# A hybrid decoder layer: compact key norms, scores over four quadrants of the array, and down biases in row groups

## The chip, the cores and the metric

One core of one Trainium2 chip. The metric is the device time of one execution of the whole layer in microseconds (us), as the median of some runs. The engines are TensorE (PE, its weight loads PEld), VectorE (DVE), ScalarE (ACT), GpSimd (POOL) and SyncE (SP), which issues nearly all DMAs.

## The reference, cut to what matters

256 tokens of width 1024 pass one layer: an RMSNorm and one projection, whose columns go to an S5 state-space mixer (512) and to an RWKV-7 mixer (r, k, v, 512 each); an output projection; a mixture of 32 experts, four for each token; an embedding gated by the residual; a last norm. The parts that the change touches:

```python
kk = heads(k * k_k)                                   # 8 heads of 64
kk = kk / jnp.maximum(jnp.sqrt(jnp.sum(kk * kk, axis=-1, keepdims=True)), 1e-12)
...
sa = jnp.einsum('bhvk,bhk->bhv', state, neg_kk_t)     # rwkv7_step, token by token
state = (state * w_t[:, :, None, :] + sa[..., None] * kka_t[:, :, None, :]
         + v_t[..., None] * k_t[:, :, None, :])
...
yb = act @ w_down[e] + b_down[e]                      # moe_ffn, for the tokens that chose e
return yb.astype(f32) * gw[:, None]
```

The kernel computes the RWKV scan in chunks of 64 tokens. Within a chunk the recurrence becomes products of 64x64 matrices ("scores") and a triangular inverse.

## The kernel before, in words

`layer` is one block in which each engine has its own instruction list in a fixed order; semaphores are the only links. At its end all engines meet, a short second block (router) follows, they meet again, and a third block loops over the experts. Its ring of eight 2 MB slots (`RING`) in SBUF is filled by SP; slots 0, 4, 5, 1 are loaded in the first block, 2, 3, 7 at the start of the second, 6 at the start of the third, and from then on a slot is refilled when the expert's matmuls have read it (`refill`, L1386).

The first block, on PE: projections 0 to 3, the small projections (`lora`), per-head sums of the squared keys (`head_sums(kksq, 4)`, two matmuls with 512 columns), projections 4 and 5, `kernel_taps`, `turn_g` (32 transposes into banks 2 to 5 that ACT copies out, L468), `stack_u` and `into` (S5), projections 6 and 7. Key norms: DVE divides with a reciprocal of all 1024 columns (L706). Then the RWKV part. A unit is one pair of heads in one chunk, 16 units in all; `pair` (L241) does two 64x64 matmuls for it, one for each head, on partitions 0 to 63 and 64 to 127, whose results lie on the same partitions of one bank:

```python
for h in range(2):
    a = slice(h * CH, (h + 1) * CH)
    last = mm(out[a], lhsT[a], rhs[a], start, stop)
```

Five sets of scores (L1008) give X, Mx, KA, RB, RK; DVE copies each out with its mask (L739). Five levels of a block inverse (L1033) follow: 16 pairs W = MO X, ACT copies them (L477), 16 pairs with Y, DVE adds them to X (L781) and transposes. `turn` (transposes of Bs, Ks, Vs) and `s5_out` (the S5 result) are placed between the levels. Then four chunks c of the scan proper (L1099) with `glu` and `project_out` in between, group norm, and the output projection. POOL splits the experts' gate and up biases into parts (L340 to L344); ACT waits for it before the last tile.

The second block: the last transposes, `ple_proj`, router logits, top four, ranks, gates; PE transposes the gates to 32 rows (L1351), and four matmuls with 32 rows and 512 columns start the output banks with the down biases (L1357). PE needs `p_in` for `ple_proj(0)`, two DMAs issued in the first block; DVE needs `router_in`, the router's bias, which SP issues first in this block (L1246).

Every fp32 matmul stands in the trace as two passes, so the counts of PE in the rows are twice those of the program.

## Time and profile before

| | |
|---|---|
| median of 3 runs | 1209.59 us (1205.43 to 1210.69) |
| the profiled execution | 1203.81 us, its span 1202.0 us |
| PE busy | 1076.2 us, 90% |
| DVE, ACT, POOL busy | 365.5, 176.3, 17.5 us |
| TensorE clock granted | 0.991 of 2.4 GHz |
| HBM read | 428.70 MB, 358 GB/s over the span |
| instructions | 18872 |

Times of rows are microseconds from the start of the span. A row of the timeline merges instructions of one line and form that follow each other: start, length, engine, line, operation, out<-in, shapes, count, and in brackets the idle time before it and what ended it.

### The profile page before, as it was taken

How to read it: one execution, taken by the hardware profiler on the slowest of the kernel's cores; microseconds unless marked ns; L12 is line 12 of the kernel's file. 1: busy time of each engine (PE TensorE's matmuls, PEld its weight loads, DVE VectorE, ACT ScalarE, POOL GpSimd, SP SyncE). 2: the span in 40 equal slices, each digit the busy share in tenths (PEclk: the TensorE clock that was granted, in tenths of full speed). 3: DMA queues.
4: the chain of work that ended last, by engine and by line, in shares of the span. 5: the costliest groups of instructions: out<-in, count | busy, mean ns of one | idle time of the engine just before them, and what ended most of it. 6: DMA issues, size and time to landing. Idle time of an engine off the chain costs nothing. (4 is left out here: it accounts for less than half of the span.)

```text
span 1202.0 us, 18872 instructions
## 1 busy us (share of the span) xinstructions
PE 1076.2 (90%) x8132; PEld 492.5 (41%) x8132; DVE 365.5 (30%) x739; ACT 176.3 (15%) x288; POOL 17.5 (1%) x18
## 2 busy tenths in 40 slices
PE   6989998899999988888888888888888888888896
PEld 5779884443334333333333333333333333333342
DVE  5997925522222111111222111111111221211122
ACT  5580231400000000000000000000000000000023
POOL 0000005000000000000000000000000000000000
PEclk9989999899999999999999999999999999999999
DMA  9301184589999999999999999999999999999970
GB/s 324 125 2 37 43 328 142 211 359 426 428 428 430 428 429 428 427 428 429 429 429 430 428 429 428 428 428 430 429 429 428 429 428 428 427 430 428 430 289 35
DMA packets 44531, 430.28 MB, mean 358 GB/s; under 512 B 4912, under 2 KB 15536, under 8 KB 19920
## 3 DMA queue, kind: packets, MB, share of 16 engines
q1 hardware_dynamic: 44304, 429.24, 85.5%
q8 instruction: 28, 0.46, 0.2%
q0 software_dynamic: 192, 0.52, 0.1%
q14 instruction: 7, 0.06, 0.0%
HBM read 428.70 MB, written 1.05 MB: 358 GB/s over the span
## 5 line engine op out<-in xcount | busy, mean ns | idle before, releaser
L1221 PE MATMUL bank<-arena 128*64 128x512 f32 (+5 forms) x5136 | 847.3, 467 | 91.0 <-DMA arena<-in_exp_w_up 58.3
L1221 PEld LDWEIGHTS bank<-arena 128*64 128x64 f32 (+4 forms) x5136 | 307.8, 128 | 607.0 <-issue 446.2
L239 PE MATMUL bank<-arena 64*64 64x64 f32 (+7 forms) x2048 | 161.6, 264 | 15.4 <-ACT arena L362 8.5
L239 PEld LDWEIGHTS bank<-arena 64*64 64x64 f32 (+3 forms) x2048 | 129.3, 144 | 45.7 <-issue 26.3
L1410 ACT ACTIVATE arena<-arena 128x512 f32<-128x512 f32 x32 | 20.1, 630 | 520.2 <-DVE arena L1458 520.2
L1463 DVE TENSOR_SCALAR arena<-bank 128x512 f32<-128x512 f32 x32 | 22.1, 691 | 227.7 <-PE bank L1221 227.7
L1473 DVE COPY arena<-bank 128x512 f32<-128x512 f32 x32 | 22.1, 691 | 202.8 <-PE bank L1221 202.8
L1458 DVE TENSOR_SCALAR arena<-bank 128x512 f32<-128x512 f32 x32 | 22.1, 691 | 194.0 <-PE bank L1221 194.0
L1413 ACT ACTIVATE arena<-bank 128x256 f32<-128x256 f32 x32 | 12.3, 383 | 326.2 <-PE bank L1517 326.2
L1434 DVE TENSOR_TENSOR arena<-bank,par 128x512 f32<-128x512 f32 x33 | 22.8, 691 | 77.9 <-PE bank L1221 77.9
L1466 DVE SCALAR_TENSOR_TENSOR arena<-arena 128x512 f32<-128x512 f32 x32 | 33.7, 1052 | 1.1
L1461 DVE TENSOR_TENSOR arena<-arena 128x512 f32<-128x512 f32 x32 | 22.1, 692 | 24.5 <-ACT arena L1410 24.5
L1415 ACT ACTIVATE arena<-bank 128x512 f32<-128x512 f32 x32 | 19.1, 597 | 1.7
L1521 PE MATMUL bank<-con,arena 128*128 128x128 f32 x128 | 19.2, 273 | 0.0
L1446 DVE TENSOR_SCALAR arena<-con,arena 128x128 f32<-128x128 f32 x64 | 19.1, 340 | 0.1
L1431 DVE TENSOR_SCALAR arena<-con,arena 128x64 bf16<-128x64 f32 x66 | 13.8, 251 | 14.3 <-PEq L1243 7.5
L1517 PEld LDWEIGHTS bank<-con,arena 128*128 128x128 f32 x64 | 6.5, 141 | 24.3 <-issue 24.3
L1521 PEld LDWEIGHTS bank<-con,arena 128*128 128x128 f32 x128 | 15.0, 140 | 0.0
L239 PE MATMUL bank<-arena,con 128*32 128x64 f32 (+1 forms) x144 | 11.4, 322 | 3.6 <-ACT arena L506 1.4
L1517 PE MATMUL bank<-con,arena 128*128 128x128 f32 x64 | 14.1, 301 | 0.0
L1410 ACT ACT_TABLE_LOAD x8 | 10.3, 1283 | 7.8 <-PEq L1243 7.7
L352 ACT ACTIVATE arena<-par 128x2048 f32<-128x2048 f32 (+1 forms) x7 | 10.3, 1533 | 0.0
(275 smaller groups left out, 406.7 us busy)
## 6 DMA issues: line engine op xcount, KB each, us to landing
arena<-in_exp_w_gate SPq DMA_DIRECT2D x64, 2048.0 KB, 32.2
arena<-in_exp_w_down SPq DMA_DIRECT2D x64, 2048.0 KB, 35.4
arena<-in_exp_w_up SPq DMA_DIRECT2D x64, 2048.0 KB, 35.3
arena<-in_w_in SPq DMA_DIRECT2D x8, 1024.0 KB, 12.9
arena<-in_w_out SPq DMA_DIRECT2D x4, 1024.0 KB, 6.3
arena<-in_ple_w_gate SPq DMA_DIRECT2D x2, 2048.0 KB, 33.4
arena<-in_xT SPq DMA_DIRECT2D x1, 1024.0 KB, 6.0
arena<-in_lora SPq DMA_DIRECT2D x1, 1024.0 KB, 13.6
```

The costliest lines, as they stand in the source:

```text
L239: return nc.tensor.matmul(out, lhsT, rhs, start=start, stop=stop, skip_group_check=True)
L1221: return nc.tensor.matmul(out, lhsT, rhs, start=start, stop=stop, skip_group_check=True)
L1410: nc.scalar.activation(sg, gt, ACT.Sigmoid, scale=1.702).then_inc(s["sig_ready"], 1)
L1415: nc.scalar.activation(actT[:, :, :, :], GATE[:, :].rearrange("p (k h s) -> p k h s", h=2, k=4), ACT.Copy).then_inc(s["actT_ready"], 1)
L1434: tt(xg[:, :, :], GAT[:, :].rearrange("p (k s) -> p k s", k=KD), prm("g_moe_run")[:, :, None].to_broadcast([P, KD, SLOTS]), ALU.mult).then ...
L1458: ts(gt, GATE[:, :], 7.0, None, ALU.min).then_inc(s["gt_ready"], 1)
L1461: tt(sg, sg, gt, ALU.mult).then_inc(s["swish_ready"], 1)
L1463: ts(up, UP[:, :], 7.0, -7.0, ALU.min, ALU.max).then_inc(s["up_read"], 1)
L1466: stt(by_run(gt), plain(up), 1.0, plain(sg), ALU.add, ALU.mult).then_inc(s["act_ready"], 1)
L1473: V.tensor_copy(y, YB[:, :]).then_inc(s["y_ready"], 1)
L1517: last = nc.tensor.transpose(YB[:, t * P:(t + 1) * P], pg[:, t, :], ident)
L1521: last = nc.tensor.transpose(GATE[:, k * P:(k + 1) * P], gt[:, k * P:(k + 1) * P], ident)
```

## The change

Three parts. *Front:* the squared keys are summed with the data as weights and two columns of ones (`head_pair`), which gives 16 columns; DVE inverts those; 16 matmuls with a broadcast weight spread them over 1024 columns again. The order of the front is new: `turn_g` in two halves behind the sums and behind the spread, `kernel_taps` behind projection 5; ACT takes a part of two token shifts, POOL two memsets. *Four quadrants:* units 8 to 15 (chunks 2 and 3) get the halves crossed, so that four 64x64 matmuls can be in different quarters of the array; this holds for scores and turns; in chunks 2 and 3 the scan crosses back, and waits (`first_half`) stand between two halves of one sum. ACT copies three score sets, POOL masks RB and RK, `phase_on(1)` moves ahead of the levels, the head sums of `rk` behind the first W, the last `s5_out` behind the last W. *Down biases:* gates and biases lie in four groups of 32 rows; the router's bias DMA counts on `p_in`, and PE waits for all three.

```diff
+        gfirst = un(9).rearrange("p (m j c) -> p m j c", m=2, c=32)
+        head_pair = head_ones[:, 0:P:CH]
+        norms, rest_mu = u0[:, 0:4 * TT * 2], u0[:, 32:32 + 2 * FT].rearrange("p (m f) -> p m f", f=FT)
-        bias_down = un(42)[0:E, :]
+        bias_down = un(42)[:, 0:D // 2]
...
-                a = slice(h * CH, (h + 1) * CH)
-                last = mm(out[a], lhsT[a], rhs[a], start, stop)
+                a, o = slice(h * CH, (h + 1) * CH), slice((h ^ cross) * CH, (h ^ cross) * CH + CH)
+                last = mm(out[o], lhsT[a], rhs[a], start, stop)
...
-                sp.dma_start(bias_down, io["exp_b_down"]).then_inc(bias_in, 16)
+                for r in range(4):
+                    hf = r % 2
+                    sp.dma_start(bias_down[r * E:(r + 1) * E, :], io["exp_b_down"][:, hf * 512:(hf + 1) * 512]).then_inc(bias_in, 16)
...
+                pool.wait_ge(s["proj_done"], at_place[0])
+                nc.gpsimd.memset(EL, 1.0).then_inc(s["pool_set"], 1)
...
+                nc.gpsimd.memset(un(2, 2), 0.0).then_inc(s["pool_set"], 1)
...
+                        pool.wait_ge(s["scores_moved"], 2 * n + b + 3)
+                        nc.gpsimd.tensor_tensor(d, d, causal, ALU.mult).then_inc(s["scores_masked"], 1)
...
+                        A(gfirst[a, m, :, o], gprod[m][a, 0], ACT.Copy)
+                        A(gpad[m][a, :, :, o].rearrange("p j n c -> p n j c"), gprod[m][a], ACT.Copy).then_inc(s["padded"], 1)
...
+                act.wait_ge(s["kk_summed"], 1)
+                A(norms, banks[6][:, 0:4 * TT * 2], ACT.Sqrt).then_inc(s["kk_norm"], 1)
...
-                    m = A(kb[:, 2 * b:2 * b + 2, :], banks[4 + b].rearrange("p (f t) -> p f t", t=T), ACT.Sqrt)
...
-                clear(2, 2)
+                for n in range(4, 8):
+                    copy_g(n)
...
+                for m, dst in ((1, Mx), (3, RB), (4, RK)):
+                    for b in range(2):
+                        act.wait_ge(s["scores_done"], 2 * m + b + 1)
+                        A(dst[:, 8 * b:8 * b + 8, :], banks[SCORE_BANK[m] + b].rearrange("p (u t) -> p u t", t=CH), ACT.Copy).then_inc(s["scores_moved"], 1)
...
-                link(ts(kb, kb, 1e-12, None, ALU.max))
-                link(V.reciprocal(kb, kb))
-                link(tt(kkn, kkn, kb, ALU.mult))
+                dve.wait_ge(s["kk_summed"], 2)
+                for b in range(2):
+                    d = kkn[:, 2 * b:2 * b + 2, :]
+                    last = tt(d, d, banks[6 + b].rearrange("p (f t) -> p f t", t=T), ALU.mult)
...
-                head_sums(kksq, 4).then_inc(s["kk_summed"], 1)
+                for n in range(4 * TT):
+                    tok = slice(n // FT * P, (n // FT + 1) * P)
+                    last = mm(banks[6][:, 2 * n:2 * n + 2], kksq[:, n % FT, tok], head_pair, True, True)
+                last.then_inc(s["kk_summed"], 1)
+                turn_g(0)
                 project(4)
+                pe.wait_ge(s["kk_norm"], 2)
+                for n in range(4 * TT):
+                    tile, f = n // FT, n % FT
+                    for h in range(2):
+                        last = mm(banks[6 + f // 2][h * CH:(h + 1) * CH, (f % 2) * T + tile * P:(f % 2) * T + (tile + 1) * P],
+                                  norms[:, 2 * n + h:2 * n + h + 1].to_broadcast([P, CH]), ident, True, True)
+                last.then_inc(s["kk_summed"], 1)
+                turn_g(1)
                 project(5)
...
+                    for u in range(8):
+                        o = slice(u * CH, (u + 1) * CH)
+                        ins = pair(banks[bank][:, o], fm(l, u), fm(r, u))
...
+                        last = pair(banks[bank + 1][:, o], fm(l, u + 8), fm(r, u + 8), cross=True)
...
-                pe.wait_ge(s["xy_ready"], 2 * LEVELS)
                 pe.wait_ge(s["turned"], 6)
                 pe.wait_ge(s["bonus_ready"], 1)
+                pe.wait_ge(s["scores_masked"], 4)
...
+                    if cross:
+                        pe.wait_ge(s["first_half"], 3 * c - 4)
                     for i, o in enumerate(tiles):
-                        last = pair(banks[0][:, o], fm(at, c * FT + i), state[:, o], False, True)
+                        last = pair(banks[0][:, o], fm(at, c * FT + i), state[:, o], False, True, cross)
...
-            sp.dma_start(rbias[:, :], io["router_b"].to_broadcast([P, E])).then_inc(s["router_in"], 16)
+            sp.dma_start(rbias[:, :], io["router_b"].to_broadcast([P, E])).then_inc(p_in, 16)
...
-            pe.wait_ge(p_in, 32)
+            pe.wait_ge(p_in, 48)
             ple_proj(0, banks[0]).then_inc(s["ple_done"], 1)
...
-            for tile in range(TT):
-                last = nc.tensor.transpose(banks[5][0:E, tile * P:(tile + 1) * P], gates[:, tile, :], ident)
+            rows = [slice(n * E, (n + 1) * E) for n in range(4)]
+            for n in range(4):
+                last = mm(banks[5][rows[n], 0:P], gates[:, n // 2, :], ident, True, True)
...
-                mm(banks[n][:, :], gatesT[:, n // 2 * P:(n // 2 + 1) * P], bias_down[:, n % 2 * HF:(n % 2 + 1) * HF], True, False)
+                mm(banks[n][:, :], gatesT[rows[n], :], bias_down[rows[n], :], True, False)
```

In the expert loop only the name of a semaphore changes (`up_read` goes, its count is added to `swish_ready`).

PE in the front, from the small projections' second part to the S5 matmuls (`arena`, `con`, `lora_hidden`, `rec` are SBUF tensors, `bank` is PSUM, counts are matmuls). Before:

```order
L239 MATMUL bank<-lora_hidden,arena 128x256 x4
L239 MATMUL bank<-arena,con 128x512 x2
L239 MATMUL bank<-arena 128x256 x32
L239 MATMUL bank<-arena 32x32 x4
...
L894 MATMUL bank<-con,arena 128x128 x32
L239 MATMUL bank<-arena,con 32x64 x64
```

and now:

```order
L242 MATMUL bank<-lora_hidden,arena 128x256 x4
L242 MATMUL bank<-con,arena 128x2 x8
L948 MATMUL bank<-con,arena 128x128 x16
L242 MATMUL bank<-arena 128x256 x16
L242 MATMUL bank<-con,rec 64x128 x16
L948 MATMUL bank<-con,arena 128x128 x16
L242 MATMUL bank<-arena 128x256 x16
L242 MATMUL bank<-arena 32x32 x4
```

The 32 transposes stood in one piece behind the taps; they now stand in two pieces of 16, each with a projection behind it.

ACT at the same place, before:

```order
L441 ACTIVATE arena<-bank 128x512 x2
L448 ACTIVATE arena<-arena 64x64x16 x4
L352 ACTIVATE arena<-par 128x2048
...
L463 ACTIVATE arena<-bank 32x16x32 x4
L468 ACTIVATE arena<-bank 128x512 x8
```

and now:

```order
L438 ACTIVATE arena<-bank 128x512 x4
L485 ACTIVATE arena<-arena 64x64x16 x4
L438 ACTIVATE arena<-bank 128x512 x4
L415 ACTIVATE arena<-bank 128x512
L490 ACT_TABLE_LOAD
```

The eight copies of `turn_g` (L468, now L438) stood behind the sine tables and the taps; they stand ahead of both, four on each side of the pads, and the memset of 2048 columns (L352) is POOL's.

PE from the fifth score set to the second level, before:

```order
L239 MATMUL bank<-arena 64x64 x160
L239 MATMUL bank<-arena,con 128x512 x2
L239 MATMUL bank<-arena 64x64 x64
L239 MATMUL bank<-arena 128x256
```

and now:

```order
L242 MATMUL bank<-arena 64x64 x192
L242 MATMUL bank<-arena,con 128x512 x2
L242 MATMUL bank<-arena 64x64 x32
L242 MATMUL bank<-arena 128x256
```

160 are the scores, 32 more the W of the first level: the two head sums of `rk` stand behind W instead of ahead of it.

## Rows read from the trace of the kernel before

**Rows 1.** The page: granted clock and DMA share in 40 equal slices.

```profile
PEclk9989999899999999999999999999999999999999
DMA  9301184589999999999999999999999999999970
```

**Rows 2.** Windows: busy time of each engine (and count), granted clock, DMA share, GB/s.

```profile
core 0: us, PE busy (x) PEld busy (x) DVE busy (x) ACT busy (x) POOL busy (x), PEclk, DMA share, GB/s
76.40:81.00 4.60, 0.05 (x1) 0.05 (x1) 4.50 (x4) 4.54 (x9) 0.00 (x0) 0.90 0.00 0
81.00:84.60 3.60, 3.60 (x20) 3.27 (x23) 3.60 (x5) 3.05 (x6) 0.00 (x0) 0.50 0.00 0
109.50:121.70 12.20, 11.45 (x325) 10.09 (x324) 10.79 (x20) 0.60 (x1) 0.00 (x0) 1.00 0.28 90
232.90:241.00 8.10, 6.46 (x8) 2.14 (x8) 0.60 (x4) 0.45 (x1) 0.00 (x0) 0.55 0.78 331
241.00:244.70 3.70, 2.74 (x49) 2.59 (x49) 0.86 (x3) 0.84 (x1) 0.00 (x0) 0.60 0.75 261
244.70:248.60 3.90, 3.90 (x18) 1.38 (x20) 1.04 (x7) 0.00 (x0) 0.00 (x0) 1.00 0.69 294
248.60:1150.00 901.40, 814.78 (x5097) 302.98 (x5094) 180.03 (x407) 59.95 (x103) 0.00 (x0) 1.00 1.01 428
```

**Rows 3.** The timeline, SP and PE: router's bias, `ple_proj(0)`, expert 0, first refill.

```profile
221.76 0.34 SPq L1246 DMA_DIRECT2D arena<-in_router_b  x1
...
222.70 1.88 PE L1221 MATMUL bank<-arena,lora_hidden 128*128 128x512 f32 x4
...
248.62 3.68 SPq L1389 DMA_DIRECT2D arena<-in_exp_w_up  x2
```

**Rows 4.** The timeline of the front: ACT's pads, PE's head sums, taps, transposes, stack.

```profile
47.78 4.29 ACT L427 ACTIVATE arena<-arena 64x1024 f32<-64x1024 f32 x4
...
56.76 1.96 PE L239 MATMUL bank<-arena,con 128*128 128x512 f32 x4 [0.91 <-ACT arena L410]
...
72.46 1.82 PEld L239 LDWEIGHTS bank<-arena 128*32 128x32 f32 x128 [0.33 <-issue]
...
74.42 1.97 PE L894 MATMUL bank<-con,arena 128*128 128x128 f32 x16
...
80.95 3.68 PE L894 MATMUL bank<-con,arena 128*128 128x128 f32 x16 [4.56 <-ACT arena L468]
...
84.56 3.10 PE L239 MATMUL bank<-arena,con 128*32 128x64 f32 x128
```

**Rows 5.** The timeline of scores and levels: DVE and ACT around PE's 64x64 matmuls.

```profile
110.74 0.69 DVE L748 TENSOR_TENSOR arena<-bank,con 128x512 f32<-128x512 f32 x1 [4.09 <-PE bank L239]
...
114.87 1.10 DVE L755 TENSOR_SCALAR arena<-arena,par 128x256 f32<-128x256 f32 x4
...
122.92 0.60 ACT L477 ACTIVATE arena<-bank 128x512 f32<-128x512 f32 x1 [12.67 <-PE bank L239]
...
129.56 3.71 PE L239 MATMUL bank<-arena 64*64 64x64 f32 x119 [1.09 <-issue]
...
133.07 2.06 PE L239 MATMUL bank<-con,arena 64*64 64x64 f32 x64
...
158.38 1.15 PE L239 MATMUL bank<-arena 64*64 64x64 f32 x32 [0.79 <-DVE arena L781]
...
158.95 1.06 ACT L483 ACTIVATE arena<-arena 128x1024 f32<-128x1024 f32 x1 [1.28 <-DVE arena L661]
```

**Rows 6.** The timeline around POOL's bias parts: DVE's group norm, tile 0 and tile 1.

```profile
198.31 2.45 POOL L343 TENSOR_TENSOR arena<-arena 32x1024 f32<-32x1024 f32 x1
...
198.81 3.64 DVE L808 TENSOR_SCALAR arena<-arena,par 128x128 f32<-128x128 f32 x4
...
207.93 1.11 DVE L808 TENSOR_SCALAR arena<-arena,par 128x128 f32<-128x128 f32 x4
```

**Rows 7.** DMA issues: the router's bias, KB each, median us from issue to landing.

```profile
arena<-in_router_b SPq DMA_DIRECT2D x1, 16.0 KB, 3.1
```

More of the change, by code:

```diff
@@ L412, in lora_out, with copy_g, rest_of_shift @@
                             last.then_inc(s["lora2_copied"], 1)
+                def copy_g(n):
+                    m, q = n // 4, n % 4
+                    act.wait_ge(s["g_turned"], n + 1)
+                    A(gturn[m][:, 4 * q:4 * q + 4, :], banks[2 + q].rearrange("p (j q) -> p j q", q=P), ACT.Copy).then_inc(s["g_copied"], 1)
+                def rest_of_shift(m, src, dst, signal):
+                    act.wait_ge(s["eps_ready"], 2)
+                    for i in range(FT):
+                        last = A(dst[:, i, :], src[:, i, :], ACT.Copy, scale=rest_mu[:, m, i:i + 1])
+                    last.then_inc(s[signal], 1)
                 copy_proj(0)
+                clear(9, 1)
                 copy_proj(1)
@@ L464, in _ @@
                 last.then_inc(s["taps_ready"], 1)
-                for m in range(2):
-                    for q in range(4):
-                        act.wait_ge(s["g_turned"], 4 * m + q + 1)
-                        A(gturn[m][:, 4 * q:4 * q + 4, :], banks[2 + q].rearrange("p (j q) -> p j q", q=P), ACT.Copy).then_inc(s["g_copied"], 1)
                 for b in range(2):
@@ L671, in token_shift, with add_shifted @@
                     return m
-                dve.wait_ge(s["proj_copied"], at_place[5])
-                dve.wait_ge(s["lora1_done"], 2)
-                link(token_shift("k", kx))
+                def add_shifted(m, name, dst):
+                    dve.wait_ge(s["shift_rest"], m + 1)
+                    for i in range(FT):
+                        last = stt(dst[:, i, 1:T], raw[name][:, i, 0:T - 1], prm("mu_" + name)[:, i:i + 1], dst[:, i, 1:T], ALU.mult, ALU.add)
+                    return last
+                link(add_shifted(0, "k", kx))
                 for i in range(FT):
@@ new lines, in _ @@
+                for b in range(2):
+                    dve.wait_ge(s["scores_done"], b + 1)
+                    d = X[:, 8 * b:8 * b + 8, :]
+                    link(tt(d, banks[SCORE_BANK[0] + b].rearrange("p (u t) -> p u t", t=CH), col(C_SU1), ALU.mult))
+                    link(tt(d, d, eye, ALU.add))
+                    turn_x(b).then_inc(s["scores_copied"], 1)
+                for b in range(2):
+                    dve.wait_ge(s["scores_moved"], b + 1)
+                    level_mask(0, b)
@@ L762, in value_and_bonus @@
+                for b in range(2):
+                    dve.wait_ge(s["scores_done"], 4 + b + 1)
+                    tt(KA[:, 8 * b:8 * b + 8, :], banks[SCORE_BANK[2] + b].rearrange("p (u t) -> p u t", t=CH), col(C_SU), ALU.mult).then_inc(s["scores_copied"], 1)
+                phase_on(1)
                 def value_and_bonus():
                     dve.wait_ge(s["proj_copied"], 8)
-                    token_shift("v", vv).then_inc(s["scaled"], 1)
+                    add_shifted(1, "v", vv).then_inc(s["scaled"], 1)
@@ L1029, in turn @@
                     pe.wait_ge(s["scaled"], 4)
-                    for b in range(2):
-                        if n:
-                            pe.wait_ge(s["turned"], 2 * n - 2 + b + 1)
-                        for u in range(8 * b, 8 * b + 8):
-                            last = pair(banks[b][:, (u % 8) * CH:(u % 8 + 1) * CH], fm((bh, kh, vv)[n], u), con[:, C_ID2:C_ID2 + CH])
-                        last.then_inc(s["turn_done"], 1)
+                    if n:
+                        pe.wait_ge(s["turned"], 2 * n)
+                    arr, eye = (bh, kh, vv)[n], con[:, C_ID2:C_ID2 + CH]
+                    for u in range(8):
+                        o = slice(u * CH, (u + 1) * CH)
+                        ins = pair(banks[0][:, o], fm(arr, u), eye)
+                        if u == 7:
+                            ins.then_inc(s["turn_done"], 1)
+                        last = pair(banks[1][:, o], fm(arr, u + 8), eye, cross=True)
+                    last.then_inc(s["turn_done"], 1)
                 for lev in range(LEVELS):
@@ L1102, in _ @@
                     for i, o in enumerate(tiles):
-                        pair(banks[0][:, o], KA[:, c * FT + i, :], Vs[:, c * FT + i, :], i == 0, False)
+                        last = pair(banks[0][:, o], KA[:, c * FT + i, :], Vs[:, c * FT + i, :], i == 0, False)
+                    if cross:
+                        last.then_inc(s["first_half"], 1)
                     if c:
@@ L1115, in _ @@
                     for i, o in enumerate(tiles):
-                        pair(banks[5][:, o], state[:, o], fm(rt, c * FT + i), False, False)
+                        last = pair(banks[5][:, o], state[:, o], fm(rt, c * FT + i), False, False)
+                    if cross:
+                        last.then_inc(s["first_half"], 1)
                     pe.wait_ge(s["u0_ready"], c + 1)
+                    pe.wait_ge(s["xy_ready"], 2 * LEVELS)
                     for i, o in enumerate(tiles):
@@ L1551, in _ @@
         def _(dve):
[L1552 removed]
+            link = chain(dve, "dve")
             def finish(t):
```

199 lines of the change are left out of this document (105 added, 94 removed).

## The prediction

> **What bounds the kernel now.** I read the slices first: the DMA share goes up and down, with slices near 0, in the first eight slices of 30 us and stays at 9 from the tenth on, while PE's clock falls below 9 in two slices only, the third and the eighth [rows 1]. The windows say what each stretch waits for. The expert loop, 248.60 to 1150.00, moves 428 GB/s at a DMA share of 1.01 with PE busy for 814.78 of 901.40 us: it is bound by transfers, and the change leaves them alone. So the loop keeps its length and moves as a whole with its first refill, which SP issues at 248.62 [rows 2, 3]. That refill waits for expert 0's first matmuls, 244.70 [rows 3], and these for everything ahead. Ahead of it PE, DVE and ACT hand work round and the DMAs have gaps, so a microsecond saved on that chain is one saved at the end, as long as the transfers keep up: in 232.90 to 248.60 they are idle for 8.10 x 0.22 + 3.70 x 0.25 + 3.90 x 0.31 = 3.9 us [rows 2].
>
> The timeline of each stretch that the diff touches comes last. In the front, PE idles 4.56 us for ACT's copies of the first 16 transposes; behind that the granted clock is 0.50, the lower level of 1.2 GHz, and the second 16 take 3.68 us where the first took 1.97 [rows 2, 4]. In the scores, DVE is busy for 10.79 of 12.20 us and PE's windows end on it: five sets of 1.9 each (as 64 passes of the turns) and the `rk` sums of 1.96 fill the time, and the first W waits for DVE's masks [rows 2, 4, 5]. In the second block the clock is at 0.55, and the four down-bias matmuls (eight passes) take 6.46 us [rows 2].
>
> Each fp32 matmul is two passes. 32 matmuls of 64x64 are 64 passes, 2.06 us [rows 5]: 64 ns for two passes, since the halves of a pair already run side by side.
>
> **A, the front: -4.4.** Removed: the idle of 4.56 (the copies now have two projections to hide behind) and, as no such idle precedes, the low clock: transposes 3.68 - 1.97 = 1.7, the S5 stack 3.10 - 1.9 = 1.2 (nearest full-clock row: 128 taps, whose weights load in 1.82) [rows 4]. Gain 7.5, by 4.56 + 2.9. Added: four more pads on ACT, a quarter as long as the four of 4.29, 1.1, with the fixed cost of four more instructions 1.3, which PE's norm sums wait for; 16 matmuls of 64x128 to spread the norms, 32 passes at about 0.11 where the two heads of a pair overlap (16 transposes are 1.97, so 0.12 each): 16 x 0.11 = 1.8; without overlap 3.5. The old sums with 512 columns, 1.96 [rows 4], are replaced by 8 with two columns and by transposes that had to be done anyway: about 0. DVE's division of 1024 columns goes; it lay beside PE's projections, so 0. ACT's shift parts, POOL's memsets: beside PE, 0. +1.3 + 1.8 - 4.6 - 2.9 = -4.4. Bounds: -7.5 (nothing added is seen) and +1 (another copy is waited for, the idle only moves).
>
> **B, scores to the first W: -4.3.** Before: 109.50 to 121.70 is 12.2 us [rows 2]. Now PE needs 0.95 for X's whole set, as four quadrants work, 0.25 of hand-over, DVE's work on X 4.1 (110.74 to 114.87, [rows 5]), 0.1, the set that reuses X's banks 0.93, 0.25, two copies on ACT 2 x 0.60 [rows 5], 0.1: 7.9. DVE no longer copies the sets on this path, and the `rk` sums (1.96 by the like row, [rows 4]) come behind W.
>
> **C, levels: -1.9.** Three turns of 2.06 go to 1.0: -3.0. The wait of 0.79 for DVE ahead of 158.38 is filled by `s5_out`: -0.8. The idle of 1.09 ahead of 129.56, which has no named releaser, goes with `phase_on(1)`: -1.1. The `rk` sums arrive: +1.9. The last `s5_out` comes late, so the gelu of 1.06 (158.95) is no longer hidden, and `glu(0)` waits for it: +1.1 [rows 5]. The chunks' `first_half` waits stand where PE changes sides: no row shows such a wait, bounds 0 and 8 x 0.33 (the "issue" gap, [rows 4]); I take one, **+0.3**, since the second half mostly starts behind other work.
>
> **D, group norm: -0.7.** Four `L808` take 3.64 while POOL's 2.45 runs, and 1.11 without [rows 6]: a stall of 2.5. As block 1 is earlier at this place, and POOL's chain hangs on other things, the overlap may be less or the same. Bounds 0 and -2.5; I take a little over a quarter, since the few us by which block 1 is earlier here are small beside POOL's whole chain.
>
> **E, the router's bias: +2.1.** PE's `ple_proj(0)` starts at 222.70. It now waits for a DMA issued at 221.76 that takes 3.1 [rows 3, 7]: 224.86, so 2.1 later, if I put its landing that way; nothing hides it, for behind it on PE stand the logits' transposes, which DVE's top four wait for. Bounds 0 (the transfer lands sooner) and 2.5.
>
> **F, down biases: -4.6.** 6.46 for eight passes is 0.81 each [rows 2]. Four groups of 32 rows side by side take as long as one matmul: 2 x 0.81, with starts 1.7. Two more small matmuls for the gates cost 0.2. 1.7 + 0.2 - 6.46 = -4.6. The taps, which lie on tiles of 32 columns, need 1.82 for 128 [rows 4], 14 ns each: tiles do run four wide; for tiles of 32 rows no row shows it. Bounds 0 and -4.8. The Trainium skill, TensorE: Matmul & The Clock Gate, Measured speedup vs the span model, gives 3.07 for four row groups with 512 columns, an estimate of 2.1 in place of 1.7; the sum would be 0.4 less. No run here shows it yet.
>
> **G, the start of expert 0: +1.0.** With 5 us less of matmuls ahead of it, the clock (0.60 in 241.00 to 244.70) may rise later. One clock level costs the 3.90 us of 244.70 to 248.60 once more at most: 0 to +3.9; a quarter, as this stretch is at 1.00 right from its start [rows 2].
>
> **H, POOL's masks and memsets beside DVE: +0.5.** In [rows 6] DVE lost about as long as POOL ran. Four masks of 512 columns, half of the 1024 that took 2.45, are 4.9: bounds 0 and 4.9. I take a tenth, since they run beside the first W, where PE has the `rk` sums to do meanwhile.
>
> **Sum:** -4.4 - 4.3 - 1.9 + 0.3 - 0.7 + 2.1 - 4.6 + 1.0 + 0.5 = **-12.0**. The profiled execution takes 1203.8 us, so 1191.8; the median shown is 1209.59, higher by 5.8, and the forecast against it is 1209.6 - 12.0 = **1197.6**. Of the 12, what falls behind the start of block 2 (E, F, G: -1.5) is under the 3.9 us that the transfers leave.
>
> **Rivals.** *R1, the quadrants stay two wide.* For it: no row shows two matmuls on the same rows of the array for different columns at 64x64; against: the 32-column taps do run that way [rows 4]. Two score sets on the path cost 0.93 more each, three turns 1.05 each: +5.0, 1202.6. What rows show of sharing is that both halves of a pair, on different rows, write the same bank within one 64 ns step [rows 5]. The Trainium skill, TensorEngine Tiling (Array Packing), Restrictions and Gotchas, says that different row tiles cannot access the same PSUM bank at once; the trace of the pairs does not agree, and so I take nothing from it. By that rule the crossed half would wait like the straight one, which is R1's time. Chance 0.13.
>
> *R2, the row groups run one after the other:* F gives +0.2 in place of -4.6: 1202.4. For it, that no row shows 32-row tiles; against, [rows 5] with 64-row tiles side by side. 0.08.
>
> *R3, slower: the clock stays low into the experts.* Now PE's 6.46 us of work at 0.55 is followed by a clock that has risen by 244.70 [rows 2]. With 1.7 us there, PE is mostly idle in block 2's end, and expert 0 could run at 1.2 GHz. An expert is 814.78/32 = 25.5 us of PE at full clock, 51 at the low one, against 901.4/32 = 28.2 of transfers: 23 us late per expert [rows 2]. It takes 12.0 to use up the gain and 18 to be slower by more than 0.5%, that is three quarters of expert 0 at the low clock: 1209.6 - 12.0 + 23 = 1220.6. Against it: expert 0 keeps PE busy without a break, and at 81.00 the low clock, too, ended within 7 us of busy PE [rows 2, 4]. 0.05.
>
> *R4, the transfers are the bound already:* a transfer behind which the refill queues keeps its place in time though the chain is earlier. With only 3.9 us of idle at the end, and shares of 0.28 and less in the scores [rows 2], savings before the ring's loads count only if these loads move up as well. Their issue waits for SBUF that the same chain frees, which speaks against. Half the gain would be lost: 1203.6, no change. 0.07.
>
> *R5, better than the sum:* the idle in A goes and nothing added is seen (3.1 more), E lands early (2.1): 1192.4. 0.05.
>
> **How the numbers follow.** The main case has 0.62, with its own spread of about 5 us either way (A's and E's bounds). The range leaves out R3 and the tails of R4 and R5: 1190 to 1205. A measurement here can tell about 0.5%, 6.05 us: faster is under 1203.5. Main, R1, R2, R5 and the lower part of R4 give faster 0.83; the other part of R4 and the upper tails same 0.12; R3 slower 0.05.
>
> **What would show it.** No idle of PE near 76 and clock at full from 80 to 88; first W some 8.7 us earlier (A and B); turns at about 1.0; `ple_proj(0)` released by the router's bias DMA about 3 us after block 2 starts; the four bias matmuls in some 1.7; first refill near 236.6; loop still 901 long. Wrong if the loop's length changes, if the turns still take 2.06, if the bias matmuls take over 3, or if the clock is low behind 235.

## The result and the profile after

The change makes the kernel slower: 1215.70 us (1207.41 to 1220.63, 20 runs) against 1207.40 us (1203.58 to 1210.69, 20 runs) in the same series, a ratio of 1.0066 with a 95% interval of 1.0053 to 1.0079. The forecast was 1197.6.

The profiled execution of the changed kernel has a span of 1215.9 us, that of before 1202.0. The first execution (1217.66 us) is 2.0 us above its kernel's median, the second (1203.81) 3.6 under its own, so the two traces differ by more (13.9) than the kernels do (8.3).

The page's slices of the changed kernel, clock and DMA share:

```profile
PEclk9997999889999999999999999999999999999998
DMA  9300166379999999999999999999999999999960
```

Before there were two slices below 9 [rows 1]; now there are four, and the fourth slice, 91 to 122 us, is at 7. Windows of the changed kernel (busy time of PE, PEld, DVE, ACT, POOL, then clock, DMA share, GB/s):

```profile
core 0: us, PE busy (x) PEld busy (x) DVE busy (x) ACT busy (x) POOL busy (x), PEclk, DMA share, GB/s
90.00:106.80 16.80, 16.80 (x72) 16.17 (x73) 9.79 (x16) 0.78 (x1) 0.00 (x0) 0.50 0.00 0
234.79:247.81 13.02, 13.02 (x31) 7.47 (x31) 6.32 (x21) 4.81 (x9) 0.00 (x0) 0.54 0.98 416
261.90:1163.30 901.40, 814.66 (x5093) 302.95 (x5090) 180.15 (x407) 59.90 (x102) 0.00 (x0) 1.00 1.01 428
```

The last line is the loop's window of [rows 2], moved by the 13.3 us by which the first refill is later: the same work at the same rate fits into it. From the first refill to the end of the span it is 954.0 us, 953.4 before, so all but 0.6 of the difference lies ahead of it. The timeline of PE (and two lines of SP) shows where; columns as in [rows 4]:

```profile
47.91 2.00 PE L242 MATMUL bank<-lora_hidden,arena 64*128 64x256 f32 x16
...
60.83 2.16 PE L242 MATMUL bank<-con,arena 128*128 128x2 f32 x16 [2.09 <-ACT arena L430]
62.86 3.35 PE L948 MATMUL bank<-con,arena 128*128 128x128 f32 x16
...
73.05 1.97 PE L242 MATMUL bank<-con,rec 128*64 128x128 f32 x32
74.94 1.97 PE L948 MATMUL bank<-con,arena 128*128 128x128 f32 x16
...
88.75 0.43 PE L242 MATMUL bank<-arena,con 128*32 128x64 f32 x16 [1.41 <-issue]
89.90 32.24 PE L242 MATMUL bank<-arena 128*128 128x64 f32 x320 [0.72 <-ACT arena L504]
...
127.63 1.49 PE L242 MATMUL bank<-arena 64*64 64x64 f32 x42 [0.17 <-ACT arena L517]
129.90 0.85 PE L242 MATMUL bank<-arena 64*64 64x64 f32 x22 [0.78 <-issue]
...
140.94 1.15 PE L242 MATMUL bank<-con,arena 64*64 64x64 f32 x62
...
154.74 1.90 PE L242 MATMUL bank<-arena 64*64 64x64 f32 x58 [0.70 <-issue]
...
158.55 7.27 PE L242 MATMUL bank<-arena 64*64 64x64 f32 x228 [0.80 <-issue]
...
167.35 1.99 PE L242 MATMUL bank<-arena 128*128 128x256 f32 x8 [1.06 <-ACT arena L527]
...
204.25 7.76 PE L242 MATMUL bank<-arena 128*128 128x512 f32 x16
213.85 10.57 PE L242 MATMUL bank<-arena 128*128 128x512 f32 x24 [1.84 <-DVE arena L865]
...
231.69 0.34 SPq L1338 DMA_DIRECT2D arena<-in_router_b  x1
...
234.79 3.78 PE L1311 MATMUL bank<-arena,lora_hidden 128*128 128x512 f32 x4 [1.99 <-DMA arena<-in_router_b]
238.37 3.46 PE L1311 MATMUL bank<-arena 128*128 128x32 f32 x16
241.63 6.18 PE L1311 MATMUL bank<-arena,lora_hidden 128*128 128x512 f32 x8
...
249.61 1.14 PE L1311 MATMUL bank<-arena 32*128 32x512 f32 x8 [0.41 <-ACT arena L1365]
...
255.72 6.78 PE L1311 MATMUL bank<-arena 128*64 128x512 f32 x20 [0.87 <-DVE arena L1526]
...
261.91 3.68 SPq L1481 DMA_DIRECT2D arena<-in_exp_w_up  x2
```

The starts of matching instructions in the two traces divide the 13.3 us by which the first refill is later (261.91 against 248.62):

| stretch, from start to start | before | after | difference | forecast |
|---|---|---|---|---|
| span's start to the small projections' second part | 45.03 | 47.91 | +2.9 | 0 |
| from there to `into` | 43.36 | 41.99 | -1.4 | -4.4 (A) |
| `into` and projections 6, 7 to the first score | 21.15 | 29.21 | **+8.1** | 0 |
| first score to first W | 12.2 | 8.5 | -3.7 | -4.3 (B) |
| first W to `glu(0)` | 38.3 | 39.7 | +1.4 | -1.9, H +0.5 |
| `glu(0)` to the last `project_out` with S5 inputs | 35.7 | 36.9 | +1.2 | +0.3 |
| from there to block 2 | 26.0 | 27.5 | +1.5 | -0.7 (D) |
| block 2's start to expert 0 | 22.9 | 24.0 | +1.1 | -2.5 (E, F) |
| expert 0 to the first refill | 3.9 | 6.2 | +2.3 | +1.0 (G) |

### The profile page after: what moved, and what is told of

Read it like the earlier page. It is cut to its first block and busy times, and to the rows that moved or that the text cites. A ratio compares the mean times of both kernels' runs of the same rounds, so it can differ in the third digit from the quotient of the medians.

```text
span 1215.9 us, 18973 instructions
## 1 busy us (share of the span) xinstructions
PE 1085.2 (89%) x8182; PEld 498.8 (41%) x8182; DVE 358.5 (29%) x726; ACT 183.1 (15%) x309; POOL 26.9 (2%) x25
## 5 line engine op out<-in xcount | busy, mean ns | idle before, releaser
L242 PE MATMUL bank<-arena 64*64 64x64 f32 (+7 forms) x2048 | 170.5, 272 | 20.5 <-ACT arena L382 8.5
L242 PEld LDWEIGHTS bank<-arena 64*64 64x64 f32 (+3 forms) x2048 | 135.4, 150 | 53.2 <-issue 35.4
L1507 ACT ACTIVATE arena<-bank 128x512 f32<-128x512 f32 x32 | 19.1, 597 | 1.7
L1523 DVE TENSOR_SCALAR arena<-con,arena 128x64 bf16<-128x64 f32 x66 | 13.9, 252 | 9.0 <-DVE arena L1544 6.8
L1311 PE MATMUL bank<-arena,lora_hidden 128*128 128x512 f32 x16 | 11.9, 900 | 2.0 <-DMA arena<-in_router_b 2.0
L415 ACT ACTIVATE arena<-bank 128x512 f32<-128x512 f32 x8 | 5.8, 720 | 35.0 <-PE bank L242 35.0
```

What stands on the lines that cost most here:

```text
L242: return nc.tensor.matmul(out, lhsT, rhs, start=start, stop=stop, skip_group_check=True)
L1311: return nc.tensor.matmul(out, lhsT, rhs, start=start, stop=stop, skip_group_check=True)
L1507: nc.scalar.activation(actT[:, :, :, :], GATE[:, :].rearrange("p (k h s) -> p k h s", h=2, k=4), ACT.Copy).then_inc(s["actT_ready"], 1)
```

## The experiments

Each run was timed against the kernel before on the same chip in the same series (medians of before 1205.5 to 1209.1), so ratios to before are what is compared across series. Two theories to begin with. **C, the clock:** PE's short idle times bring the low level, and what PE does there counts double. **W, the waits:** what is lost are the added waits and the clash of POOL and DVE themselves.

### The router's bias gets its own wait again

```diff
-            sp.dma_start(rbias[:, :], io["router_b"].to_broadcast([P, E])).then_inc(p_in, 16)
+            sp.dma_start(rbias[:, :], io["router_b"].to_broadcast([P, E])).then_inc(s["logits_done"], 16)
...
-            act.wait_ge(s["logits_done"], 1)
+            act.wait_ge(s["logits_done"], 17)
...
-            dve.wait_ge(p_in, 48)
-            dve.wait_ge(s["logits_done"], 1)
+            dve.wait_ge(s["logits_done"], 17)
...
-            pe.wait_ge(p_in, 48)
+            pe.wait_ge(p_in, 32)
```

> The changed kernel, but PE's ple_proj(0) waits only for the two early DMAs, as before, and DVE alone waits for the router's bias. Theory C (the clock): in the changed kernel PE idles 1.99 us for this DMA and the granted clock is at the low level from there on, so that ple_proj and the logits take 3.78 + 3.46 + 6.18 = 13.4 us where they took 7.5 before; with the wait gone both go: 1215.7 - 2.0 - 5.9 = about 1208. Theory W (the wait itself): only the 2.0 go, the clock falls anyway: about 1213.7. No effect: 1215.7.

Measured: 1208.62 us, ratio 1.0022 (1.0008 to 1.0036), so 0.0044 or some 5 us under the changed kernel's. The trace, PE in the second block:

```profile
234.18 1.88 PE L1311 MATMUL bank<-arena,lora_hidden 128*128 128x512 f32 x4
236.17 1.97 PE L1311 MATMUL bank<-arena 128*128 128x32 f32 x16
237.98 3.68 PE L1311 MATMUL bank<-arena,lora_hidden 128*128 128x512 f32 x8
```

The wait is gone and the 13.4 us are 7.5 again. A wait of 2 us cost about 5 (3 to 8 by the two intervals): C, not W, which had 2.

### POOL's masks go to DVE

```diff
-                for n, dst in enumerate((RB, RK)):
-                    for b in range(2):
-                        d = dst[:, 8 * b:8 * b + 8, :]
-                        pool.wait_ge(s["scores_moved"], 2 * n + b + 3)
-                        nc.gpsimd.tensor_tensor(d, d, causal, ALU.mult).then_inc(s["scores_masked"], 1)
...
+                    if lev in (1, 2):
+                        for b in range(2):
+                            d = (RB, RK)[lev - 1][:, 8 * b:8 * b + 8, :]
+                            dve.wait_ge(s["scores_moved"], 2 * lev + b + 1)
+                            tt(d, d, col(C_UI), ALU.mult).then_inc(s["scores_masked"], 1)
```

> The changed kernel, but DVE masks RB and RK, in the second and third level, where it has idle time, and POOL does nothing in the scores. In the changed kernel DVE's operations beside POOL's four masks took 1.64 to 1.76 us in place of 0.69. Theory P (POOL and DVE hinder each other): some 4 us of DVE come back, of which about 3 lie on the path: about 1212.7. Rival: DVE had slack there, the added masks (4 x 0.69) cost as much: 1215 to 1217.

Measured: 1215.04 us, 1.0062 (1.0040 to 1.0085): no change against 1.0066. The clash is real. In the changed kernel a DVE operation beside POOL's masks takes 1.76 us:

```profile
127.24 6.48 POOL L352 TENSOR_TENSOR arena<-arena,con 128x512 f32<-128x512 f32 x4 [68.36 <-ACT arena L517]
127.48 1.76 DVE L708 TENSOR_TENSOR arena<-arena 128x512 f32<-128x512 f32 x1
```

In this run DVE's operations are back to 0.69 us, but DVE then waits for PE instead:

```profile
130.14 0.69 DVE L789 TENSOR_TENSOR arena<-arena,con 128x512 f32<-128x512 f32 x1 [0.49 <-PE bank L242]
133.14 0.69 DVE L829 TENSOR_TENSOR arena<-arena,bank 128x512 f32<-128x512 f32 x1 [2.31 <-PE bank L242]
```

Theory P falls: no cost of H can be seen in the time.

### The crossing is switched off

```diff
-                a, o = slice(h * CH, (h + 1) * CH), slice((h ^ cross) * CH, (h ^ cross) * CH + CH)
+                a, o = slice(h * CH, (h + 1) * CH), slice(h * CH, (h + 1) * CH)
```

> The changed kernel with the crossing switched off: the halves of units 8 to 15 go to the same side as those of units 0 to 7, everything else (order, waits between halves of a sum, ACT copies) stays. Theory Q (four quadrants do work side by side, as the turns' 1.15 us in place of 2.03 say): three turns and two score sets go back to two wide, +3 and +1.8: about 1220. Rival (the waits of the scan and DVE eat the gain, or PE is not the bound there): 1215 to 1217.

Measured: 1218.20 us, 1.0092 (1.0061 to 1.0122), against 1.0066: +3, but the intervals overlap. In the trace the turns are back at the old length:

```profile
147.15 2.03 PE L242 MATMUL bank<-con,arena 64*64 64x64 f32 x64
```

1.15 against 2.03 us shows four 64x64 matmuls side by side. From the first score to the first W this trace takes 10.2 us where the changed kernel takes 8.5, so the crossing wins 1.7 there, as the theory says. From the first W to `glu(0)` it takes 39.4 us, and the changed kernel 39.7: the 2.6 us that three shorter turns save do not show. PE has 1.07 us of idle there with straight halves and 3.34 with crossed ones. What the quadrants are worth was asked again without the new front (below).

### The row groups alone, in the kernel before

```diff
+            rows = [slice(n * E, (n + 1) * E) for n in range(4)]
+            for n in range(4):
+                last = mm(banks[5][rows[n], 0:P], gates[:, n // 2, :], ident, True, True)
...
-                mm(banks[n][:, :], gatesT[:, n // 2 * P:(n // 2 + 1) * P], bias_down[:, n % 2 * HF:(n % 2 + 1) * HF], True, False)
+                mm(banks[n][:, :], gatesT[rows[n], :], bias_down[rows[n], :], True, False)
```

with the four DMAs and POOL's count of 192 as in the change.

> The kernel before with the down biases in four row groups as the only change (the router's bias keeps its own semaphore). The changed kernel's trace shows 1.14 us for the four where before it was 6.46, so -5.3, and +0.1 for two more small matmuls: 1207.4 - 5.2 = about 1202. Rival: with less work for PE ahead of the experts the clock rises later, and the first expert gives back 2 to 4 us: 1204 to 1206.

Measured: 1204.53 us, 0.9989 (0.9974 to 1.0005): almost nothing won. In the trace the eight passes are down to 1.50 us, but the group norm ahead of them is late:

```profile
205.44 12.26 PE L239 MATMUL bank<-arena 128*128 128x512 f32 x24 [2.40 <-DVE arena L813]
...
236.14 1.50 PE L1223 MATMUL bank<-arena 32*128 32x512 f32 x8 [0.40 <-ACT arena L1275]
```

Before, this wait was 1.16 and the 24 passes took 10.57. POOL waits for all bias DMAs, the four for the down biases among them, although it never reads these. The rival that was named for this run shows as well: from expert 0's start to the first refill this trace takes 5.9 us, 3.9 before, at a low clock that before fell on the down biases.

### POOL no longer waits for the down biases

One edit, on the kernel with the row groups alone and on the changed kernel with its router wait mended:

```diff
-                    sp.dma_start(bias_down[r * E:(r + 1) * E, :], io["exp_b_down"][:, hf * 512:(hf + 1) * 512]).then_inc(bias_in, 16)
+                    sp.dma_start(bias_down[r * E:(r + 1) * E, :], io["exp_b_down"][:, hf * 512:(hf + 1) * 512]).then_inc(p_in, 16)
...
-                pool.wait_ge(bias_in, 192)
+                pool.wait_ge(bias_in, 128)
...
-            pe.wait_ge(p_in, 32)
+            pe.wait_ge(p_in, 96)
```

> e4_bias_alone (the kernel before with row groups alone), and POOL no longer waits for the down biases. In e4 the second block came 3.2 us later than before (PE idle 2.40 for DVE, then 12.26 for 10.57 at a low clock), which ate the 5.0 won by the row groups. Theory L: these 3.2 come back: 1204.5 - 3.2 = about 1201.3. Rival: the loss has another cause: 1204.5.

> e1_router_wait, and POOL starts its bias parts when the gate and up biases are there, no longer waiting for the four DMAs of the down biases (they count on the semaphore that PE waits for in the second block). Theory L (late POOL): in e1 PE idles 2.90 us for DVE L865 and its next 24 passes take 13.50 us in place of 10.57, since POOL's 1024-column operations now lie on tile 0's group norm; earlier POOL gives back 1.7 of idle and the 2.9 of low clock: about 4.5 under e1, 1204. Rival: POOL's chain is long enough (15 us) to meet the group norm either way: within 1 us of e1, 1208.6.

Measured, old front: 1203.66 us, 0.9967 (0.9951 to 0.9982); with 0.9989 ahead of it, 2.7 us came back, and the row groups are worth 4.0 us (2.2 to 5.9) once POOL is out of the way. The 2.7 are no more than an estimate, since the intervals overlap, and not all of it need be POOL's: in the two traces 3.0 us are won ahead of the second block, but expert 0 is also back at 3.9 us. Changed kernel: 1209.08 us, 1.0006 (0.9990 to 1.0021), 1.9 less than e1, with overlapping intervals too. There the group norm still meets POOL, as these rows of DVE and POOL show, first of the changed kernel, then of e5:

```profile
205.14 2.12 POOL L363 TENSOR_TENSOR arena<-arena 64x1024 f32<-64x1024 f32 x1
...
205.25 2.56 DVE L860 TENSOR_TENSOR arena<-arena 128x512 f32<-128x512 f32 x1
207.84 4.49 DVE L862 TENSOR_SCALAR arena<-arena,par 128x128 f32<-128x128 f32 x4
```

```profile
187.09 1.04 POOL L360 CAST arena<-arena 128x1024 bf16<-128x1024 f32 x1 [61.43 <-DMA arena<-in_exp_b_up]
...
198.61 4.50 DVE L862 TENSOR_SCALAR arena<-arena,par 128x128 f32<-128x128 f32 x4
```

POOL starts when its DMAs land, and these are issued behind three of the ring's loads: its start follows the issue of the first of these loads by 30.8 us before and in e8, 32.0 in e4, 31.7 in e5 and 32.4 in the changed kernel, while DVE's first 128x512 operation of the group norm follows it by 42.3 before and 41.4 in e5 and the changed kernel. The two come closer from both sides: the two operations take 2.56 + 4.49 us now, 1.10 + 3.64 before. D had the wrong sign.

### Projection 6 between the stack and its products

```diff
                 stack_u()
+                project(6)
                 into(0)
                 into(1)
-                project(6)
```

> e1_router_wait with projection 6 between the S5 stack and its products (into), so that PE has work while ACT copies the stacked inputs. Theory C (idle of PE brings the low clock, seen for 13 us behind these gaps in all traces of the new front): the idle of 0.72 us goes and with it the stretch at the low clock, some 7 us: about 1201. Rival F (the low clock comes from the small matmuls or from the 1.1 us without a named releaser ahead of it, which stays): -0.7 alone, 1208.

Measured: 1208.45 us, 1.0003 (0.9989 to 1.0016), 2.3 us under e1's, with intervals that overlap. The clock is at full level from 86 to 116 us in its trace, as C says, although an idle of 1.65 us without a named releaser still stands in the stack (rival F). Yet PE now waits for DVE, which got the S5 products 7 us later:

```profile
115.96 3.33 PE L242 MATMUL bank<-arena 64*64 64x64 f32 x128 [2.83 <-DVE arena L688]
123.98 5.23 PE L242 MATMUL bank<-arena 64*64 64x64 f32 x192 [4.69 <-DVE arena L801]
```

What the clock gave back, a new wait took.

### Filler in the two gaps around the stack

```diff
+                for n in range(2):
+                    mm(banks[6][:, :], ident, hT[:, 0:2, :], True, True)
                 stack_u()
+                mm(banks[6][:, :], ident, hT[:, 0:2, :], True, True)
                 into(0)
```

> e1_router_wait with three added matmuls of 512 columns whose results nobody reads, two ahead of the S5 stack and one behind it: 2.6 us of PE work in the place of two gaps of 1.1 and 0.7 us. Theory C: the clock stays at full level in the two projections behind it, which go from 21 + 8 us to 21: about 7 under e1, 1202. Rival: the clock falls whatever PE does there: e1 + 1, about 1209.6.

Measured: 1204.49 us, 0.9964 (0.9944 to 0.9984). Three matmuls that compute nothing of use make the kernel 0.0058, or 7 us, faster than e1. The trace:

```profile
83.40 4.96 PE L242 MATMUL bank<-arena,con 128*128 128x512 f32 x134
88.20 24.08 PE L242 MATMUL bank<-arena 128*128 128x64 f32 x320
```

The gaps are gone, and the 320 passes that took 32.24 in the changed kernel and 30.74 in e1 take 24.08. Across all traces: with this filler (five kernels) the clock is at 1.00 from 86 to 104 us in every one. Without it, with the same order of work, it is at 0.50 to 0.55 from 92 to 104 in five of six; e5's execution is the exception, though its gaps are the same (0.94 and 0.74). Its twelve times fall in two groups, 1203.4 and 1203.8, and ten from 1207.7 on. In the five traces that have the stretch, it lasts 14 to 17 us, with PE busy. So the gap makes the low stretch likely, not certain.

### Filler in the old front

Five such matmuls in the 4.55 us that PE waits for ACT's copies, in the kernel before with mended row groups:

```diff
+                        if n == 4:
+                            for i in range(5):
+                                mm(banks[6][:, :], ident, hT[:, 0:2, :], True, True)
                         if n >= 4:
                             pe.wait_ge(s["g_copied"], n - 3)
```

> e8_bias_pool_early with five matmuls of 512 columns, nobody's input, in the 4.55 us in which PE waits for ACT's copies of the first 16 transposes. Theory C (idle of PE brings the low clock): transposes 3.68 to 1.97, stack 3.06 to 1.9: e8 - 2.9. Rival (the clock falls there for another cause): e8 or a little over it.

```profile
76.73 4.46 PE L239 MATMUL bank<-arena,con 128*128 128x512 f32 x10
81.45 2.13 PE L899 MATMUL bank<-con,arena 128*128 128x128 f32 x16 [0.27 <-ACT arena L470]
83.51 1.99 PE L239 MATMUL bank<-arena,con 128*32 128x64 f32 x128
```

The low clock is gone there, and the 3.67 and 3.06 us of e8 became 2.13 and 1.99, as C says. The time was 1203.06 us, 0.9979 (0.9957 to 1.0001), not better than e8: eight runs lie from 1198.7 to 1203.1, four from 1208.8 to 1209.7. The slower four were not profiled. That a low stretch comes later in them, where the first one used to be, is a guess.

### The quadrants alone

The scores, turns and scan of the change, on the kernel of e8, with the old front and DVE's copies:

```diff
+                        ins = pair(banks[bank][:, o], fm(l, u), fm(r, u))
+                        if u == 7:
+                            ins.then_inc(s["scores_done"], 1)
+                        last = pair(banks[bank + 1][:, o], fm(l, u + 8), fm(r, u + 8), cross=True)
```

> e8_bias_pool_early (the front and the DVE copies of before) with the four quadrants alone: scores and turns with crossed second half, scan of chunks 2 and 3 crossed back with its waits. Turns 2.03 to 1.15 us, three of them: -2.6; scores little, since DVE copies all five sets as before: 0 to -1; the scan's waits +0.5: about e8 - 2.5, 1201 in the frame of 1203.7. Rival: in block 1's later part POOL's meeting with the group norm takes it back: e8.

Measured: 1204.24 us, 0.9978 (0.9961 to 0.9995), e8 had 0.9967: no gain.

```profile
120.13 3.75 PE L239 MATMUL bank<-arena,con 128*128 128x512 f32 x4 [0.20 <-DVE arena L754]
...
142.19 1.15 PE L239 MATMUL bank<-con,arena 64*64 64x64 f32 x64
145.11 6.25 PE L239 MATMUL bank<-arena 128*128 128x256 f32 x198 [1.77 <-DVE arena L663]
```

Turns are at 1.15, but PE waits for DVE right behind one, and `glu(0)` comes at 161.06 where e8 has it at 160.33. The two sides of the first W differ. Behind it, up to `glu(0)`, e11 takes 37.2 us for e8's 38.8: 1.5 are won. Ahead of it, from the first score, e11 takes 14.0 us for 12.2: where DVE sets the pace, matmuls twice as fast buy idle time (1.21, 1.06 and 1.06 us between 112 and 118), and behind this idle the clock is at 0.50 from 118 to 124.8 us, so that the `rk` sums take 3.75 us where e8 has 1.96. In the changed kernel the crossing helps in the scores (1.7 us by e3); that it does so because ACT took three of the five copies is likely, but no run separates it.

### Repairs together, and what is left

Router wait, filler and POOL's start in one kernel:

> The changed kernel with three repairs: own wait for the router's bias (e1), filler around the stack (e7), POOL's start without the down biases (e5). If the three are independent, e7's ratio to before, 0.9964, improves by what e5 did to e1, 0.0016: 0.995, about 1201.5. Rival: POOL and group norm still meet, since POOL starts when its DMAs land and block 1 is now earlier: as e7.

Measured: 1201.73 us, **0.9958** (0.9940 to 0.9975): faster than both kernels. It is not clearly faster than e8, which has the row groups without the new front and the quadrants (0.9967, 0.9951 to 0.9982). To it, POOL's second half behind the group norm:

```diff
                 for m in range(2):
+                    if m:
+                        pool.wait_ge(s["mix_rw_ready"], 2)
```

> e9_three_repairs with POOL's second half (the up biases' parts) moved behind both tiles of the group norm. In e5 DVE's group norm of tile 0 took 1.81 + 4.50 us for two operations that take 0.69 + 1.11 in tile 1, PE idled 2.73 us and then ran 24 passes at 12.26 in place of 10.57. Theory L: DVE gives back some 4 us of which 2.2 are on the path, and 1.7 of clock, less what POOL now disturbs behind it: 3 under e9. Rival: the disturbance moves to the second norm (both tiles' sums, on the path too) and nothing is won.

Measured: 1203.01 us, 0.9971 (0.9954 to 0.9987). PE's wait for the group norm is gone from the trace and the first refill comes at 245.71 instead of 246.78, but the time is no better; inconclusive.

Then filler in more gaps: two matmuls ahead of the norm sums and three ahead of the last `project_out` (e13), and two more behind the down biases (e14), each of this form:

```diff
+            for n in range(2):
+                mm(banks[7][:, :], ident, con[:, 0:512], True, True)
```

> e9_three_repairs with filler in two more places: two matmuls of 512 columns while PE waits for ACT's pads (2.09 us idle at 58), three while it waits for the group norm (2.76 us idle at 203). Theory C: the transposes behind the first go 3.35 to 1.97 and the norm's broadcast and projection lose the rest of their low clock (0.3), the 24 passes behind the second 12.26 to 10.57: 3.4 under e9, about 1198.3 where e9 is 1201.7. Rival (the low clock has other causes there): e9 + 0 to 0.5.

> e13 with two more such matmuls between the down biases and expert 0, where PE waits for DVE (1.71 and 0.86 us). Theory C: expert 0's first products go from 18.2 to 16.3 us, and the first refill comes up to 1.9 sooner: e13 - 1.5. Rival: the transfers' gap is used up there, or the clock falls for another cause: e13 within 0.5.

Measured: e13 1205.57 us, 0.9978 (0.9962 to 0.9993), no gain over e9; its trace has 10.57 us behind the group norm, but the transposes are still at 2.60 although PE idled only 0.39 ahead of them. Covering the gap but for these 0.39 us was not enough. e14: 1202.55 us, 0.9955 (0.9938 to 0.9973), 3.0 under e13 in the same series, with intervals that overlap. Its windows around the first refill, 242.49:

```profile
229.00:236.00 7.00, 4.24 (x27) 1.79 (x26) 2.70 (x14) 2.00 (x4) 0.00 (x0) 1.00 0.99 425
236.00:242.50 6.50, 5.51 (x68) 2.88 (x70) 1.94 (x9) 0.86 (x1) 0.00 (x0) 1.00 0.98 405
```

The clock is full, and the transfers have no gap left. Its span of 1198.6 ends 956.1 us behind the first refill where the changed kernel and e8 take 954.0 and 953.4: here the earlier refill is not worth its whole lead. That is R4's mechanism, and of all traces this one alone shows it; the other sixteen lie between 953.2 and 954.0.

### The changed kernel once more

No edit.

> The changed kernel itself once more, for a second trace. Theory C: the stretch at the low clock behind the S5 stack is there again in the trace (projections 6 and 7 with the products between them near 29 to 31 us in place of 21), ratio to before 1.0066 as at first. If it was chance: full clock there and a ratio nearer 1.000.

Measured: 1216.87 us, 1.0077 (1.0055 to 1.0099), and in the trace:

```profile
86.27 0.43 PE L242 MATMUL bank<-arena,con 128*32 128x64 f32 x16 [1.26 <-issue]
87.41 32.39 PE L242 MATMUL bank<-arena 128*128 128x64 f32 x320 [0.72 <-ACT arena L504]
```

The stretch is there again: the 320 passes take 32.39 us, with the clock at 0.50 from 88.1 to 105.0. The profiled execution, 1211.9 us, is the shortest of the six. What is not there is the late start: the small projections' second part begins at 45.55, not 47.91. So that part of the first table, +2.9, does not come in every execution: the first 16 passes took from 5.10 to 6.71 us over the traces, by when the clock first rose (the passes start 0.43 us apart until then and 0.22 from then on), and behind the idle of 3.03 us that follows them the clock is low again in some. Whether the change has a part in it stays open: of the twelve traces with the new front six begin there at 47.6 us or later, of the five with the old one none.

## Why the prediction was wrong

**What bounds the kernel** was right: from the first refill to the end all traces but e14's take 953.2 to 954.0 us, so the end moved one for one with the first refill.

**A, the step that failed.** It said that the low clock goes, since the idle of 4.56 that preceded it goes. The idle went, the clock's low stretch did not: it moved. Shorter idle times stand now at other places, 2.09 ahead of the norm sums, which are followed by transposes at 3.35 instead of 1.97, and 1.41 and 0.72 around the stack, which are followed by some 17 us at 0.50. Before, such a stretch fell on transposes and the stack and cost 2.6 (e12's trace against e8's, 2.9 by the prediction); now it falls on two projections that PE works through without a break, and costs 8.1. Filler shows the place (7 us between e1 and e7). The prediction took a clock penalty as tied to one gap; it priced a new one only ahead of the experts (G). Apart from the clock, A's steps were about right: spread 1.97 for 1.8, second transposes 1.97. In its own stretch A came to -1.4 for -4.4, since the first transposes ran at the low clock and the stack lost its shorter passes again to the idle of 1.41, which was not in the sum.

**B** -3.7 for -4.3: right.

**C** was wrong by 3.3 us. The turns took 1.15 where 1.0 was forecast, but what they saved (-3.0 in the sum) went into idle of PE without a named releaser: 0.70 ahead of 154.74 and 0.80 ahead of 158.55. The old idle of 1.09, which C took out with `phase_on(1)`, is there again as 0.78 ahead of 129.90. With straight halves, e3, the stretch takes no longer, 39.4 us for 39.7. The gelu's wait (1.06) and the `rk` sums (1.98) came at full price. With the old front, e11, the quadrants brought no gain in the time: 1.5 us won behind the first W, 1.8 lost to the low clock ahead of it.

**D** had the wrong sign, -0.7 forecast, +1.5 measured in the stretch. POOL's start hangs on DMAs behind the ring's loads, which do not get faster with the engines, and on three more DMAs in the change. Without the four for the down biases it starts 1.2 us sooner (30.8 for 32.0), and e8 is 2.7 us under e4, an estimate within the noise.

**E** was sized right (1.99 for 2.1) and too small in its effect: the 2 us of idle took the clock down under the 7.5 us of PE work behind it, 5.9 more. In the trace that is 7.9 together; e1 gives 5 us (3 to 8).

**F** right in mechanism: eight passes took 1.14 us for 1.7, since by then the clock had risen; worth 4.0 us alone (e8, with POOL's wait taken out) for 4.6.

**G** +2.3 for +1.0, inside its bounds. Expert 0's start to the first refill takes 3.9 us in five traces and 5.7 to 6.6 in twelve, and e4 has the longer time with the row groups as its only change. **H** did not show in the time (e2), though DVE's operations did get longer.

**The rivals.** R1 and R2 did not happen: turns at 1.15, row groups at 1.14. R3 named the cause, a low clock that follows a thinner stretch of PE work, and put it in the wrong place: the first expert lost 2.3 us, while block 1's projections and block 2's logits carried it. It had 0.05, because I asked only whether the clock would stay low where it is low now, not where the change opens new idle.

Of the 8.3 us, then: about 5 are the router's wait with its clock and 7 the stretch behind the stack, and these two are shown by e1 and e7; some 2 may be POOL's late start, which no pair of runs shows clear of its noise; against them stand the 4 of the row groups and the scores' gain. With the three mended, the change gives 0.9958; the row groups alone give 0.9967 (e8), so a gain of the new front and the quadrants is not shown. Open: why the low stretch is missing in some executions (e5) and present after a nearly covered gap in another (e13).

## What to carry to other kernels

An idle microsecond of TensorE is priced with what follows it: list every gap that a change opens, and put the work behind it at the low clock, for the 3 to 17 us that such stretches lasted here, as the bad case of the sum. When a stage gets faster, look for what in it is started by a transfer and will not move along. And keep waits apart: a DMA that counts on a semaphore of another, or a consumer that waits for bytes that it never reads, adds no line of work; the first cost some 5 us here, the second by estimate 2.7.

## What the runs showed of the hardware

- Three idle-filling matmuls of 0.85 us made the kernel 0.58% faster (e7 against e1). The low clock is the 1.2 GHz level, 0.50 in the windows, and one stretch of it lasted at least 16.8 us with PE busy for the whole time (90.0 to 106.8, changed kernel).
- Four 32-row matmuls of 512 columns (eight passes) took 1.14 us in the changed kernel, where eight passes with 128 rows take 3.68 in e1: 3.2 times. The Trainium skill, TensorE: Matmul & The Clock Gate, Measured speedup vs the span model, has 3.07; the trace agrees.
- Crossed and straight pairs of 64x64 run together: 64 passes take 1.15 us in the changed kernel, against 2.03 in e3, with two row tiles writing one bank. The rule of the Trainium skill, TensorEngine Tiling (Array Packing), Restrictions and Gotchas, that different row tiles cannot access the same bank at once, would have left the crossed turns at 2.03; these traces do not agree with it.
- DVE operations beside POOL's two-input ones took 1.64 to 1.76 us for 0.69 (changed kernel against e2), and four of 128x128 took 4.49 in the changed kernel, 1.11 in [rows 6] without POOL.
